# Layer 0 of a hybrid decoder step: decode states, cache rows and decode queries put between the units of the latent prompt attention

## The chip, the cores and the metric

The kernel runs on one core of a Trainium2 chip. The metric is device time in microseconds (us) of one launch. The kernel before was timed three times: 3633.6 us in the median, 3632.26 to 3640.36.

A core has four compute engines, each with its own list of instructions that it works off in order: TensorE (PE: matmuls and transposes, results in PSUM), VectorE (DVE), ScalarE (ACT) and GpSimd (POOL, here mostly a queue for indirect DMAs). SyncE (SP) issues the other DMAs. Engines wait for each other by semaphores. PSUM has eight banks of 128 x 512 float32, here `ps[:, 0]` to `ps[:, 7]`.

## The reference

One inference step of a two-layer trunk over a prompt of 1024 tokens and 8 decode tokens (one for each of 8 running sequences). The change lies in layer 0, which runs latent attention (MLA, 8 heads) beside gated linear attention (GLA, 4 heads), for the prompt and for the decode tokens:

```
q_pe  = rope(q[..., 64:], pos)
q_lat = einsum('bqhc', q[..., :64], w_uk)            # queries into the latent space
c_kv  = rms_norm(kv_a[..., :256]); k_pe = rope(kv_a[..., 256:])
rows  = concat([c_kv, k_pe])                         # cache rows, an output (prompt and decode)
keys  = rows                     (prompt)   or  concat([cache[page_table], rows])   (decode)
mla   = softmax(scale * (q_lat . c_kv + q_pe . k_pe), causal) . c_kv . w_uv
o, s_fin = gla_chunked(gq, gk, gv, log_a, s0)        # s = exp(last) * s + k^T v;  s_fin is an output
o     = rms_norm(o, g_norm) * silu(g_r)
out   = concat([mla, o]) @ w_out
```

For a decode token GLA is one step: the state read from memory is scaled by the decay, the outer product of key and value is added (`s_fin`), and the output is the query times the new state.

## The kernel before, in words

All data live in one SBUF array (`arena`). `NT` = 8 is the number of 128-token tiles, `NH` = 8 the heads of MLA, `DEC` = 8 the decode tokens, `SEQ` = 1024, `T` = 1032. Instructions are written in program order, engine by engine; there is no scheduler. `link` makes an engine wait for its own last result; `enter(e, k)` makes it wait until every engine has reached phase k, and `leave` counts the phase up: an engine barrier.

Layer 0 runs, after the input projection, in these parts:

- `pe_gla` and its partners: 16 steps of the GLA recurrence over the prompt, with the projections of the MLA queries between them (`QH`). After each chunk `gnorm(n)` normalises its output: ScalarE squares, TensorE sums over partitions in bank 7 (line 1051), ScalarE takes Ln and Exp, each of which loads its own function table (lines 1062 and 1064), and VectorE multiplies (1069, 1073).
- Then, one after the other: the decode keys (two transposes, 1154; VectorE spreads them by token, 1185), `gnorm(7)`, 4 value units (`pe_mla_values`, 1280: a tile of 128 tokens times `w_uv`, into banks 6 and 7, copied by VectorE at 1287), the decode states (16 matmuls, 1167, over banks 1 to 4, each followed by two VectorE operations, 1195), 4 more value units, the decode outputs (32 matmuls of one column, 1177), the cache rows (9 tiles, three transposes each, 1220 and 1221, copied at 1241 and sent out by SP), the decode queries (24 matmuls, 1225), the transposed new row (1230), and `gnorm(8)` for the decode tokens.
- Phase 8, a barrier of all engines, then `pe_mla`, `act_mla`, `dve_mla`: the prompt attention. POOL passes the same barrier and issues the first two page gathers of the decode attention behind it.
- Phase 9, the decode attention over the paged cache (`pages`).

The attention works through `MU`, 64 units (head, query tile), in the order 0, 7, 1, 6, 2, 5, 3, 4 of the query tiles, so small and large units take turns. Unit u with query tile i has i + 1 key tiles. Its steps are: `scores(u)` (TensorE, banks 0 and 1 or 2 and 3, line 1311), `mask(u)` (VectorE adds the causal mask and takes the maximum, 1404, 1407), the exponential (ScalarE, 1375), `turn(u)` (TensorE transposes the weights into banks 4 and 5, 1323), `finish(u)` (VectorE copies them into the single buffer `PT`, 1421), `values(u)` (TensorE, bank 6 or 7, 1335) and the output (ScalarE, 1371). TensorE issues, for each u, `scores(u + 1)`, `turn(u)`, `values(u - 1)`. Keys of a head (`keys(h)`, four matmuls of 128x512, 1296, copied at 1394) use banks 4 and 5 too. The names `turn(1)`, `scores(0)` and so on below mean these steps with their unit number, over all heads: u = 8 is the first unit of the second head.

SP issues in layer 0, in this order: GLA's prompt states, the decode states, the eight prompt row tiles, the decode row, and then (after the scores of the decode attention) the input again and the weights of the next projection.

## Time and profile before

| | us |
|---|---|
| median of three timed runs | 3633.6 |
| the profiled execution, its own time | 3640.52 |
| its span in the trace | 3638.7 |
| TensorE matmul busy | 3399.5 (93%) |
| VectorE busy | 1668.2 (46%) |
| ScalarE busy | 630.5 (17%) |
| mean granted TensorE clock | 0.968 |

The profile is one execution. Times within it count from the start of the span. PE is TensorE's matmuls, PEld its weight loads, which overlap them. A float32 matmul leaves two records in the trace, so counts of records are twice the counts of instructions. Clock is what the throttle granted to TensorE as a share of 2.4 GHz. In a timeline row the first number is the start, the second how long the group lasted; `[1.13 <-ACT ...]` is the idle time of that engine before it, and what ended it.

### The profile page before, as it was taken

Reading aid. Unit: us, or ns where it says so; the run is one execution under the profiler, and the core shown is the slowest. Engines: PE = TensorE matmul, PEld = TensorE weight load, DVE = VectorE, ACT = ScalarE, POOL = GpSimd, SP = SyncE. Lnnn points to the kernel's source line nnn. Section 1 sums busy time; section 2 is a strip of 40 time slices with the busy share of each in tenths; the row PEclk is TensorE's granted clock in tenths of the full one; section 3 lists DMA queues with packets and bytes.
Section 4 is the critical chain, followed back from the end, with each engine's and each line's share of the span. In section 5 each row is a group of like instructions: output and inputs, shape, how many; then the busy total and the mean of one; then the engine's idle time right before and its main releaser. Section 6 shows DMA issues by size and latency. Waiting matters only on the chain. (4 is left out here: it accounts for less than half of the span.)

```text
span 3638.7 us, 45085 instructions
## 1 busy us (share of the span) xinstructions
PE 3399.5 (93%) x18216; PEld 2510.8 (69%) x18216; DVE 1668.2 (46%) x3894; ACT 630.5 (17%) x1628; POOL 95.0 (3%) x138
## 2 busy tenths in 40 slices
PE   9999888766889999999999999999987999999997
PEld 5675565654557777776777767767764777777676
DVE  0216455688254333357760212122456433335777
ACT  1214223233130000000030111111223000000002
POOL 0000000011000000000000000000220000000000
PEclk9999799899899999999999999999988999999998
DMA  3120100298321111111221111122210111011122
GB/s 134 35 58 1 46 33 1 108 351 325 128 82 47 46 37 43 46 61 64 78 87 46 60 56 55 56 73 69 79 67 23 47 46 46 35 46 61 64 89 100
DMA packets 63531, 266.58 MB, mean 73 GB/s; under 512 B 6288, under 2 KB 24728, under 8 KB 52352
## 3 DMA queue, kind: packets, MB, share of 16 engines
q1 hardware_dynamic: 55072, 176.94, 14.0%
q0 software_dynamic: 8288, 87.30, 6.4%
q8 instruction: 114, 1.87, 0.2%
q14 instruction: 57, 0.47, 0.0%
HBM read 246.29 MB, written 17.93 MB: 73 GB/s over the span
## 5 line engine op out<-in xcount | busy, mean ns | idle before, releaser
L512 PE MATMUL ps<-arena 128*128 128x344 f32 (+1 forms) x4928 | 1083.1, 383 | 22.4 <-ACT arena L560 12.0
L512 PEld LDWEIGHTS ps<-arena 128*128 128x128 f32 x4928 | 833.6, 192 | 272.6 <-issue 26.0
L766 PE MATMUL ps<-arena 128*128 128x344 f32 (+1 forms) x2464 | 539.8, 382 | 1.5 <-DVE arena L685 1.5
L766 PEld LDWEIGHTS ps<-arena 128*128 128x128 f32 x2464 | 415.3, 191 | 126.7 <-DVE arena L685 3.4
L1945 PE MATMUL ps<-arena 128*128 128x344 f32 x1152 | 354.3, 465 | 15.6 <-ACT arena L352 5.7
L1945 PEld LDWEIGHTS ps<-arena 128*128 128x128 f32 x1152 | 221.3, 195 | 134.7 <-issue 26.3
L216 PE MATMUL ps<-arena 128*128 128x344 f32 x672 | 198.5, 459 | 8.9 <-DMA arena<-in_w_a 8.9
L1956 PE MATMUL ps<-arena 128*128 128x256 f32 (+1 forms) x864 | 206.4, 396 | 0.0
L1956 PEld LDWEIGHTS ps<-arena 128*128 128x128 f32 (+1 forms) x864 | 178.9, 264 | 23.5 <-issue 6.2
L562 ACT ACTIVATE arena<-arena 128x688 f32<-128x688 f32 (+1 forms) x88 | 55.7, 633 | 756.5 <-DVE arena L624 756.5
L216 PEld LDWEIGHTS ps<-arena 128*128 128x128 f32 x672 | 129.8, 194 | 76.8 <-DMA arena<-in_w_a 8.9
L1656 DVE STREAM_TRANSPOSE arena<-arena 128x1152 f32<-128x1152 f32 x128 | 167.6, 1352 | 21.9 <-DMA arena<-in_cache,arena 21.9
L1530 PE MATMUL ps<-arena 128*32 128x128 f32 x2304 | 77.2, 293 | 56.1 <-DVE arena L1656 56.1
L2094 ACT ACTIVATE arena<-arena 128x128 f32<-128x128 f32 (+1 forms) x192 | 84.0, 438 | 244.6 <-DVE arena L2137 244.6
L2132 DVE CUSTOM_DVE_ANT_0 arena<-ps,arena 128x128 f32<-128x128 f32 (+1 forms) x192 | 56.1, 348 | 136.0 <-PE ps L2052 89.3
L374 PE MATMUL ps<-arena 128*128 128x344 f32 x384 | 115.0, 462 | 0.8 <-DVEq L155 0.8
L1530 PEld LDWEIGHTS ps<-arena 128*32 128x32 f32 x2304 | 67.5, 119 | 64.5 <-DVE arena L1656 63.7
L2000 DVE COPY arena<-ps 128x344 f32<-128x344 f32 x36 | 18.5, 516 | 194.1 <-PE ps L1945 194.1
L374 PEld LDWEIGHTS ps<-arena 128*128 128x128 f32 x384 | 74.6, 195 | 40.0 <-issue 2.4
L598 DVE TENSOR_TENSOR arena<-arena 128x512 f32<-128x512 f32 x44 | 30.4, 692 | 151.9 <-DMA arena<-in_w_fi 151.9
L621 DVE TENSOR_TENSOR arena<-arena,ps 128x344 f32<-128x344 f32 (+1 forms) x88 | 37.2, 423 | 109.0 <-PE ps L512 109.0
L624 DVE TENSOR_TENSOR arena<-arena,ps 128x344 f32<-128x344 f32 (+1 forms) x88 | 37.2, 423 | 108.9 <-PE ps L512 108.9
(322 smaller groups left out, 3662.0 us busy)
## 6 DMA issues: line engine op xcount, KB each, us to landing
arena<-in_w_fi SPq DMA_DIRECT2D x44, 1024.0 KB, 4.8
arena<-in_w_fo SPq DMA_DIRECT2D x16, 1536.0 KB, 6.4
arena<-in_w_fo SPq DMA_DIRECT2D x16, 1280.0 KB, 5.7
arena<-in_w_out_a SPq DMA_DIRECT2D x24, 512.0 KB, 3.5
arena<-in_w_qk SPq DMA_DIRECT2D x24, 512.0 KB, 3.6
arena<-in_c SPq DMA_DIRECT2D x6, 2048.0 KB, 12.3
arena<-in_x SPq DMA_DIRECT2D x6, 1376.0 KB, 10.3
arena<-in_w_a SPq DMA_DIRECT2D x14, 512.0 KB, 3.5
```

The source lines that it names most:

```text
L216: mm = pe.matmul(ps[:, 3 * u + c, 0:C], w[:, k, :], X[:, k, chunk(c)], start=(k == 0), stop=(k == KD - 1))
L374: mm = pe.matmul(ps[:, 3 * u + s // 2 % 3, 0:C], w[:, k, :], rhs(k)[:, chunk(c)], start=(k == 0), stop=(k == kt - 1))
L512: mm = pe.matmul(ps[:, BANK[p], 0:HALF[s]], prod[j][p][0], prod[j][p][1], start=(j == 0), stop=(j == 3))
L562: act.activation(GATE[:, 0:2 * HALF[s]], GATE[:, 0:2 * HALF[s]], ACT.Silu).then_inc(st_g, 1)
L621: dve.tensor_tensor(v, u, bank["p7"], ALU.add).then_inc(st_e, 1)
L766: mm = pe.matmul(ps[:, BANK[p], 0:HALF[s]], prod[p][0], prod[p][1], start=(j == 0), stop=(j == NKP - 1))
L1530: mm = pe.matmul(ps[32 * j:32 * j + 32, n % 2, 0:P], QBD[n // NG % 2][:, cb, :], KVT[(4 * n + j) % 8][:, :, cb * 32:cb * 32 + 32], start=( ...
L1656: dve.transpose(KVT[(4 * n + q) % 8], KV[n % 4][:, 4 * q:4 * q + 4, :]).then_inc(kt_done, 1)
L1945: mm = pe.matmul(ps[:, b, 0:C], w[:, k, :], X[:, k, chunk(c)], start=(k == 0), stop=(k == KD - 1))
L1956: mm = pe.matmul(ps[0:P if tt < NT else DEC, b, 0:256], X[:, k, block_slice(g, tt)], w[:, k, :], start=(k == 0), stop=(k == KD - 1))
L2094: act.activation(DS[n % 2][:, j, 0:nk], DS[n % 2][:, j, 0:nk], ACT.Exp, bias=DMX[:, n % 2, j:j + 1], scale=DIL_SCALE, accum_out=s[:, 260 + ...
L2132: dve.tensor_tensor_reduce(DS[n % 2][:, j, 0:nk], ps[:, j % 2, off:off + nk], BIAS[i % 2][:, j, 2 * P - nk:2 * P], 1.0, NEG, ALU.add, ALU. ...
```

## The change

The barrier in front of phase 8 is gone: after GLA TensorE goes straight on with `keys(0)`. All steps on decode states, cache rows and decode queries move out of the stretch in front of the attention and become fills inside it. `FILL` lists them: `("keys", 0)`, 8 times `state`, 2 times `out`, `norm`, 9 times `row`, `query` and `new`, 23 entries. Entry k stands at unit u = 2k + 2, behind `values(u - 1)` on TensorE and behind `finish(u)` on VectorE; ScalarE's part of the norm stands behind the exponential of the odd unit after it.

So that the attention keeps banks 0 to 6, all fills share bank 7, and `values(u)` has bank 6 alone, so it waits for the output of u - 1 (before: of u - 2). A state step handles one token: two matmuls into bank 7, four VectorE operations. The decode outputs are two steps of 16 matmuls. The decode queries of GLA are copied to a small place (`GQD`) first, since the attention's output `O` goes over them; the key buffers `KH` and the row buffers `KVROW` have new places. The value units (6, then 2) and `gnorm(7)` stand in front of scores(0), between keys(0) and keys(1). The page gathers wait for nine output transfers (GLA's prompt states, decode states, and the decode row) in place of the barrier and eight.

```diff
         def pe_gla_decode_keys(pe):
-            pe.wait_ge(g_atc, NGLU)
+            pe.wait_ge(gn_r, NT)
+            pe.wait_ge(v_cp, NT)
             for pr in range(2):
-                mm = pe.transpose(ps[0:DEC, 0, pr * P:pr * P + P], gk[:, pr, SEQ:T], ident[:, :])
+                mm = pe.transpose(ps[0:DEC, 7, pr * P:pr * P + P], gk[:, pr, SEQ:T], ident[:, :])
...
+        def pe_gla_decode_state(pe, b):
+            pe.wait_ge(gs_km, b + 1)
+            if b:
+                pe.wait_ge(gs_stc, 2 * b)
+            for pr in range(2):
+                pe.matmul(ps[:, 7, 2 * pr * P:2 * pr * P + 2 * P], KM[0:DEC, b, pr * P:pr * P + P],
+                          GV[0:DEC, NT, 2 * pr * P:2 * pr * P + 2 * P], start=True, stop=True).then_inc(gs_st, 1)
+        def pe_gla_decode_out(pe, hh):
+            pe.wait_ge(gs_stc, 2 * DEC)
+            if hh:
+                pe.wait_ge(gs_o, 2)
+            r = slice(64 * hh, 64 * hh + 64)
+            for pr in range(2):
+                for b in range(DEC):
+                    mm = pe.matmul(ps[:, 7, pr * DEC + b:pr * DEC + b + 1], SG[r, b, pr, :], GQD[r, pr, b:b + 1],
+                                   start=True, stop=True)
+            mm.then_inc(gs_o, 1)
...
+        FILL = [("keys", 0)] + [("state", b) for b in range(DEC)] + [("out", 0), ("out", 1), ("norm", 0)]
+        FILL += [("row", tt) for tt in range(NT + 1)] + [("query", 0), ("new", 0)]
+        def fill_at(u):
+            return FILL[u // 2 - 1] if u % 2 == 0 and 0 < u // 2 <= len(FILL) else ("", 0)
...
             def values(u):
-                if u >= 2:
-                    pe.wait_ge(m_oc, u - 1)
+                if u:
+                    pe.wait_ge(m_oc, u)
...
             keys(0)
+            pe.wait_ge(gn_r, NT - 1)
+            pe_mla_values(pe, range(6))
+            pe.wait_ge(v_cp, 6)
+            pe_gnorm(pe, NT - 1)
+            pe.wait_ge(kh_cp, 1)
+            keys(1)
+            pe.wait_ge(gn_r, NT)
+            pe_mla_values(pe, range(6, NT))
+            scores(0)
             for u, (h, i) in enumerate(MU):
...
                 if u:
                     values(u - 1)
+                fill(*fill_at(u))
...
+                if u and fill_at(u - 1) == ("out", 1):
+                    act.wait_ge(gs_o, 4)
+                    act_gnorm_squares(act, NT)
+                if u and fill_at(u - 1) == ("norm", 0):
+                    act_gnorm(act, NT)
...
             for u, (h, i) in enumerate(MU):
                 if u + 1 < len(MU):
                     mask(u + 1)
                 finish(u)
+                fill(*fill_at(u))
+                if u and fill_at(u - 1) == ("norm", 0):
+                    link("dve", dve, dve_gnorm(dve, NT))
...
             pool.wait_ge(pidx_ok, NG)
-            enter(pool, 8)
-            pool.wait_ge(out_done, 16 * 8)
+            pool.wait_ge(out_done, 16 * 9)
             gather(0)
```

Where the instructions stand. TensorE before, from the end of GLA to the first row tiles (1154 decode keys, 1051 norm, 1280 values, 1167 states, 1177 outputs, 1220 and 1221 rows):

```order
152 L1041 MATMUL ps<-arena 128x256
153 L1154 MATMUL ps<-arena 8x128 x2
154 L1051 MATMUL ps<-arena 128x512
155 L1280 MATMUL ps<-arena 128x512 x8
156 L1167 MATMUL ps<-arena 128x256 x16
157 L1280 MATMUL ps<-arena 128x512 x8
158 L1177 MATMUL ps<-arena 128x1 x32
159 L1220 MATMUL ps<-arena 128x128 x2
160 L1221 MATMUL ps<-arena 128x32
161 L1220 MATMUL ps<-arena 128x128 x2
162 L1221 MATMUL ps<-arena 128x32
```

and, further on in the same list, from the last row to the first turn (1225 queries, 1230 new row, 1296 keys, 1311 scores, 1323 turn):

```order
175 L1220 MATMUL ps<-arena 8x128 x2
176 L1221 MATMUL ps<-arena 8x32
177 L1225 MATMUL ps<-arena 96x8 x16
178 L1225 MATMUL ps<-arena 64x8 x8
179 L1230 MATMUL ps<-arena 96x8 x3
180 L1051 MATMUL ps<-arena 128x32
181 L1296 MATMUL ps<-arena 64x512 x4
182 L1311 MATMUL ps<-arena 128x128
183 L1296 MATMUL ps<-arena 64x512 x4
184 L1311 MATMUL ps<-arena 128x512 x2
185 L1323 MATMUL ps<-arena 128x128
```

TensorE after, the whole way from the end of GLA to the first turns (1309 is keys, 1293 values, 1324 scores, 1336 turn, 1348 values(u)):

```order
152 L1041 MATMUL ps<-arena 128x256
153 L1309 MATMUL ps<-arena 64x512 x4
154 L1293 MATMUL ps<-arena 128x512 x12
155 L1051 MATMUL ps<-arena 128x512
156 L1309 MATMUL ps<-arena 64x512 x4
157 L1293 MATMUL ps<-arena 128x512 x4
158 L1324 MATMUL ps<-arena 128x128
159 L1324 MATMUL ps<-arena 128x512 x2
160 L1336 MATMUL ps<-arena 128x128
161 L1324 MATMUL ps<-arena 128x256
162 L1336 MATMUL ps<-arena 128x128 x8
163 L1348 MATMUL ps<-arena 128x64
```

Everything between the last GLA matmul (1041) and keys(0) has left; the values and the norm come behind keys(0), and 25 matmuls stand between GLA and scores(0).

TensorE after, around the first state steps (1157 decode keys, 1165 a state step, units u = 2 to 4):

```order
166 L1336 MATMUL ps<-arena 128x128 x2
167 L1348 MATMUL ps<-arena 128x64 x8
168 L1157 MATMUL ps<-arena 8x128 x2
169 L1324 MATMUL ps<-arena 128x384
170 L1336 MATMUL ps<-arena 128x128 x7
171 L1348 MATMUL ps<-arena 128x64 x2
172 L1324 MATMUL ps<-arena 128x512
173 L1324 MATMUL ps<-arena 128x256
174 L1336 MATMUL ps<-arena 128x128 x3
175 L1348 MATMUL ps<-arena 128x64 x7
176 L1165 MATMUL ps<-arena 128x256 x2
```

Each fill stands between the values of the odd unit before it and the scores of the next but one.

VectorE before, from the last GLA norm but one to the second block of values (1069 and 1073 norm, 1183 and 1185 decode keys, 1287 value copies, 1195 states):

```order
148 L1069 SCALAR_TENSOR_TENSOR arena<-arena 128x512
149 L1073 TENSOR_TENSOR arena<-arena 128x4x128
150 L1183 COPY arena<-ps 8x256
151 L1185 TENSOR_SCALAR arena<-arena 8x256 x8
152 L1069 SCALAR_TENSOR_TENSOR arena<-arena 128x512
153 L1073 TENSOR_TENSOR arena<-arena 128x4x128
154 L1287 COPY arena<-ps 128x512 x4
155 L1195 SCALAR_TENSOR_TENSOR arena<-arena,ps 64x128 x32
156 L1287 COPY arena<-ps 128x512 x4
```

VectorE after, around the decode keys (1480 the copy of the turned weights, 1181 and 1183 the decode keys, 1191 a state step, 1463 and 1466 the mask, 1475 the reciprocal):

```order
175 L1480 COPY arena<-ps 128x256
176 L1181 COPY arena<-ps 8x256
177 L1183 TENSOR_SCALAR arena<-arena 8x256 x8
178 L1463 ISA arena<-ps,arena 128x384
179 L1463 ISA arena 128x1
180 L1466 TENSOR_SCALAR arena<-arena 128x1
181 L1475 RECIPROCAL arena<-arena 128x1
182 L1480 COPY arena<-ps 128x896
183 L1463 ISA arena<-ps,arena 128x768
184 L1463 ISA arena 128x1
185 L1466 TENSOR_SCALAR arena<-arena 128x1
186 L1475 RECIPROCAL arena<-arena 128x1
```

The nine operations of the decode keys now stand in front of mask(4); before they stood in front of `gnorm(7)` and all value copies.

## Rows read from the trace of the kernel before

**Rows 1.** Windows by stage: length, busy time (instructions) per engine, clock, DMA, GB/s

```profile
385.00:447.00 62.00, 54.27 (x214) 33.78 (x211) 28.35 (x73) 8.19 (x11) 0.00 (x0) 0.67 0.14 39
447.00:489.00 42.00, 36.72 (x141) 22.78 (x142) 18.07 (x47) 9.29 (x25) 2.54 (x2) 0.77 0.28 113
489.00:517.00 28.00, 24.78 (x141) 16.69 (x140) 15.09 (x41) 8.77 (x24) 0.00 (x0) 1.00 0.00 1
517.00:685.00 168.00, 151.19 (x856) 104.70 (x855) 91.53 (x245) 52.43 (x143) 0.00 (x0) 0.97 0.00 1
```

**Rows 2.** Timeline, GLA's end: start, us, engine, line, op, idle before

```profile
384.21 0.83 PE L1041 MATMUL ps<-arena 128*128 128x256 f32 x2 [1.55 <-ACT arena L1087]
...
386.21 2.08 PE L1051 MATMUL ps<-arena 128*128 128x512 f32 x2 [0.75 <-ACT arena L1056]
...
391.01 9.04 PE L1280 MATMUL ps<-arena 128*128 128x512 f32 x16 [2.72 <-ACT arena L1064]
...
394.83 0.69 DVE L1287 COPY arena<-ps 128x512 f32<-128x512 f32 x1 [2.36 <-PE ps L1280]
```

**Rows 3.** Timeline, decode and cache steps up to the attention

```profile
387.82 2.18 DVE L1185 TENSOR_SCALAR arena<-arena 8x256 f32<-8x256 f32 x8
...
399.98 11.60 PE L1167 MATMUL ps<-arena 8*128 8x256 f32 x32
...
400.78 11.79 DVE L1195 SCALAR_TENSOR_TENSOR arena<-arena,ps 64x128 f32<-64x128 f32 x32
...
420.47 6.75 PE L1177 MATMUL ps<-arena 64*128 64x1 f32 x64
...
428.01 0.69 PE L1220 MATMUL ps<-arena 128*128 128x128 f32 x2
...
428.88 0.69 PE L1220 MATMUL ps<-arena 128*128 128x128 f32 x2
...
436.35 7.08 PE L1225 MATMUL ps<-arena 64*96 64x8 f32 x48
...
444.68 1.28 ACT L1064 ACT_TABLE_LOAD   x1
445.97 0.23 ACT L1064 ACTIVATE arena<-arena 128x32 f32<-128x32 f32 x1
...
446.99 6.56 PE L1296 MATMUL ps<-arena 128*64 128x512 f32 x8 [2.65 <-DVEq L2756]
```

**Rows 4.** Timeline, scores(1) and turn(1) of the first head

```profile
458.85 1.99 PE L1311 MATMUL ps<-arena 96*128 96x512 f32 x4
...
463.62 1.97 PE L1323 MATMUL ps<-arena 128*128 128x128 f32 x8 [2.25 <-ACT arena L1375]
```

**Rows 5.** Windows, turn(1) to the next keys, first and second head

```profile
463.62:488.73 25.11, 23.38 (x115) 18.55 (x115) 11.74 (x32) 7.50 (x21) 0.00 (x0) 0.74 0.00 1
497.08:516.63 19.55, 17.46 (x115) 13.44 (x115) 11.66 (x32) 7.47 (x22) 0.00 (x0) 1.00 0.01 1
```

**Rows 6.** Timeline, TensorE's waits in the second head

```profile
497.08 1.09 PE L1323 MATMUL ps<-arena 128*128 128x128 f32 x8 [1.13 <-ACT arena L1375]
...
514.07 0.74 PE L1323 MATMUL ps<-arena 128*128 128x128 f32 x5 [0.67 <-DVE arena L1421]
...
516.63 3.65 PE L1296 MATMUL ps<-arena 128*64 128x512 f32 x8 [0.98 <-DVE arena L1421]
```

**Rows 7.** Windows of 2 us around changes of the granted clock

```profile
384.00:386.00 2.00, 1.26 (x4) 0.52 (x4) 0.81 (x3) 0.99 (x4) 0.00 (x0) 0.66 0.00 0
394.00:396.00 2.00, 2.00 (x4) 0.79 (x4) 0.69 (x1) 0.00 (x0) 0.00 (x0) 0.78 0.00 0
422.00:424.00 2.00, 2.00 (x27) 2.00 (x27) 0.00 (x0) 0.00 (x0) 0.00 (x0) 1.00 0.00 0
424.00:426.00 2.00, 2.00 (x22) 2.00 (x22) 0.00 (x0) 0.00 (x0) 0.00 (x0) 0.90 0.00 0
440.00:442.00 2.00, 2.00 (x15) 1.98 (x15) 0.00 (x0) 0.00 (x0) 0.00 (x0) 0.50 0.00 0
```

More of the change, by code:

```diff
@@ L1331, in values, with fill @@
                     pe.wait_ge(v_cp, NT)
-                if u >= 2:
-                    pe.wait_ge(m_oc, u - 1)
+                if u:
+                    pe.wait_ge(m_oc, u)
                 for j in range(i + 1):
-                    mm = pe.matmul(ps[:, 6 + u % 2, 0:64], PT[:, j * P:(j + 1) * P], V[:, j, h * 64:h * 64 + 64],
+                    mm = pe.matmul(ps[:, 6, 0:64], PT[:, j * P:(j + 1) * P], V[:, j, h * 64:h * 64 + 64],
                                    start=(j == 0), stop=(j == i))
                 mm.then_inc(m_o, 1)
-            keys(0)
+            def fill(what, x):
+                if what == "keys":
+                    pe_gla_decode_keys(pe)
+                if what == "state":
+                    pe_gla_decode_state(pe, x)
+                if what == "out":
+                    pe_gla_decode_out(pe, x)
+                if what == "norm":
+                    pe_gnorm(pe, NT)
+                if what == "row":
+                    pe_cache_row(pe, x)
+                if what == "query":
+                    pe_decode_query(pe)
+                if what == "new":
+                    pe_decode_row(pe)
+            pe.wait_ge(q_act, 3 * NH)
+            pe.wait_ge(q_dve, 3 * NH)
+            keys(0)
+            pe.wait_ge(gn_r, NT - 1)
[6 more added lines that the diff above has]
+            pe_mla_values(pe, range(6, NT))
+            pe.wait_ge(g_atc, NGLU)
+            pe.wait_ge(g_oc, NGLU)
+            pe.wait_ge(g_stc, NGLU)
+            scores(0)
             for u, (h, i) in enumerate(MU):
-                if u == 0:
-                    scores(0)
-                    pe.wait_ge(kh_cp, 1)
-                    keys(1)
                 if u + 1 < len(MU):
@@ L1388, in dve_mla, with fill @@
             for q in range(2):
-                dve.wait_ge(row_out[q], 16 * (NT // 2))
-            for q in range(2):
                 dve.tensor_copy(KH[q][64:96, :], PB[64:96, T_MISC, 0:SEQ]).then_inc(kh_pe, 1)
+            dve.tensor_copy(GQD, gq[:, :, SEQ:T])
+            def fill(what, x):
+                if what == "keys":
+                    dve_gla_decode_keys(dve)
+                if what == "state":
+                    dve_gla_decode_state(dve, x)
+                if what == "out":
+                    dve_gla_decode_out(dve, x)
+                if what == "row":
+                    dve_cache_row(dve, x)
+                if what == "query":
+                    dve_decode_query(dve)
+                if what == "new":
+                    dve_decode_row(dve)
             def keys(h):
@@ L2643, in _ @@
             pe_gla(pe)
[L2644 to L2654 removed]
             pe.sem_inc(phase["pe"], 8)
[L2656 to L2658 removed]
+            pe_mla(pe)
+            enter(pe, 9)
+            pe_pages(pe)
             enter(pe, 10)
```

171 lines of the change are left out of this document (68 added, 103 removed).

## The prediction

> **What bounds the kernel now.** I read the windows by stage first, then the timeline of layer 0 from the end of the gated linear attention (GLA) into the latent prompt attention, then the granted clock around it. The change touches the stretch from 385 to 685 us only, and there TensorE sets the pace in all of it: it is busy 54.3 of 62 us between the GLA and the attention, and 151 of 168 us in the attention [rows 1]. But the first stretch is busy at a mean clock of 0.67 and the rest at 0.97 to 1.00 [rows 1]. As the clock has two levels (1.0 is 2.4 GHz, 0.5 is 1.2 GHz), 0.67 means that about 41 of the 62 us ran at half speed. So the stretch holds three kinds of time: work that the attention needs first (16 value matmuls), decode and cache work that nothing in the prompt attention reads, and idle time at hand-overs.
>
> GLA's last matmul ends at 385.04 [rows 2]; turn(1), the first transposes of a large unit, starts at 463.62 [rows 4]. I use turn(1) as the mark, since from it on both kernels run the same loop.
>
> **The prologue: what goes.** Between the marks lie 78.6 us. They hold the norm's matmul at 386.21 and the idle stretch to 391.01 [rows 2]; decode states 11.6 us; decode outputs 6.75 us; nine cache rows at 0.86 us each (the distance of two) at half clock; decode queries 7.1 us; then a tail without dense work, from 443.4 to 446.95, in which ScalarE loads a table and all engines meet [rows 3]; and keys(0) at half clock, 6.56 us instead of 3.65 [rows 3, 6].
>
> **The prologue after.** TensorE's list is keys(0), six value units, the norm's matmul, keys(1), two value units, scores(0), scores(1). At full clock keys take 3.65 us, in 8 records (two for each 128x512 float32 matmul), so 0.43 us a record when they follow each other [rows 6]; a value unit is two matmuls, 4 records, 1.71 us. Nothing holds keys(0) back: its queries are done in GLA. Sum: keys 2 x 3.43 = 6.9; values 8 x 1.71 = 13.7; norm 0.9. One wait is exposed: the norm's matmul writes bank 7, so it waits for the copy of value 5, about 0.9 us (the copy is 0.69 us [rows 2], the rest is the hand-over). The next wait, ScalarE's Ln and Exp on that norm, was 2.7 us of TensorE idle at 391.01 [rows 2]; now keys(1), 3.4 us, lies under it. The clock fell at the end of GLA (0.66 in 384 to 386) and rose 3.9 us after dense matmuls began at 391.01 [rows 2, 7]. I assume the same: 3.9 us at half from 385, which costs 2.0. So scores(0) start at 385.1 + 6.9 + 13.7 + 0.9 + 0.9 + 2.0 = 409.5, and scores(1) at 409.9. Before, scores(1) started at 458.85 and turn(1) 4.77 us later [rows 4]; that piece (mask, exp, then the idle 2.25 us) does not change. turn(1): about 414.6. **Gain of the prologue: 49 us.** Bounds: clock full at once, 51; clock half through all of it, 23 us of work twice as long, 49 - 21 = 28. I take the row's 3.9 us, as the list is dense 128-row work like that at 391.
>
> **The loop: what comes.** A fill stands behind values(u-1) at each even u. Its work on TensorE is paid in full unless TensorE waited next. In a head at full clock (19.55 us from turn(1) to the next keys [rows 5]) the waits are 1.13 us in front of the turn of the second unit, 0.67 in front of the last unit's, and 0.98 in front of keys [rows 6]; a fill at u%8=0 lies under the first, one at u%8=6 under the second. Fills at 2 and 4 lie under nothing. Terms:
> - 8 state steps at u = 4 to 18: two matmuls of 256 columns, each half of a keys matmul, 0.91 us per step. Gross 7.3. Hidden: twice 0.67 and twice 0.91, 3.2. VectorE's four operations (0.37 each, 11.79/32 [rows 3]) come in front of the next mask and PT copy; laid into a head they push the copy by 0.2 to 0.4 us, 8 x 0.25 = 2.0. The first steps run at half clock, +0.9. Net 7.0.
> - keys step, u = 2: two transposes 0.6 us; VectorE's 2.2 us [rows 3] fall where TensorE is slow. 0.6.
> - two output steps: 64 records, 27 in 2 us at full clock [rows 7], 4.7 us; 0.67 hidden. 4.1.
> - norm step: ScalarE loads two tables, 1.28 us each [rows 3], with two short operations 3.1 us, in front of the exp of u = 26 and of VectorE's norm, which stands before mask(27). Between 0 (the exp of u = 26 is small and early) and 3.1 (all of it late) I take 1.3, as a small unit's exp is wanted only after a large unit's turn and values.
> - 9 row steps at u = 26 to 42: 0.43 us (half of 0.86), 3.9; four lie under waits. 2.2.
> - query step, u = 44: 48 records at 27 in 2 us, 3.6, nothing hides it. (At half clock it took 7.1 [rows 3].) The last step, 0.2, is hidden.
> Sum 18.8 us. The single output bank adds a wait of values(u) for output(u-1), but ScalarE does that output right after exp(u+1), and turn(u+1), at least 0.3 us, stands between. I cost it at 0; if it came out it would be 0.3 us in 64 units, 19.
>
> The ACT_TABLE_LOAD is also where a page speaks against the change: "ScalarE: Activation LUTs" of the Trainium skill, section on what the load costs, puts 1.38 us of drain behind each, 2.66 in all. The row shows the next ACTIVATE 0.01 us after the load ends (444.68 + 1.28, 445.97 [rows 3]). By the page the norm step would cost 2.8 us more; I follow the row.
>
> **The clock in the loop.** The decode outputs started at full clock and it fell 5 us into them (0.90 in 424 to 426), and it stayed at 0.50 while they, the rows and the queries kept TensorE busy 2.00 of 2.00 us [rows 7]. So small matmuls (few rows or columns) don't hold the clock, busy or not. An output step is 2.4 us and the query step 3.6, shorter than those 5, with attention between. One half-clock spell is priced by the first head: 25.11 us at a mean clock of 0.74 against 19.55 at 1.00, thus 5.6 us for 13 us at half, 0.43 us per us [rows 5]. That spell began in the idle of turn(1), and I leave it in both kernels. I add one spell of 9 us for the outputs or the query, 4 us. "TensorE: Matmul & The Clock Gate" in the Trainium skill (What's actually happening) says that busyness releases the throttle. By that alone I would add nothing; the row at 440 to 442, busy and at half, disagrees.
>
> **DMA and POOL.** The first two page gathers wait now for nine output transfers, the last of which (the new cache row) goes out at u = 42 of 64. Some 22 units at 3.5 us, 77 us, remain before the pages stage. The gathers are the DMA of 447 to 489, 0.28 of 42 us, 12 us [rows 1]. Hidden, cost 0. SP has in front of the pages stage only output transfers, so its later queue is not late.
>
> **Sum.** 49 - 18.8 - 4 = 26, with a unit of doubt in each step; I take 27, as the fill at u%8=6 also shortens the idle that ends heads, before two of which the clock fell (0.97 in 517 to 685 [rows 1]). The profiled execution took 3640.5 us (span 3638.7 and 1.8 around it), so 3613.5 by its own measure. It is 6.9 us above the median of the timed runs, 3633.6, which gives **3607 us** for the median.
>
> **Rivals.**
> 1. *The clock doesn't hold (ends slower).* Fills of 8-row and 1-column matmuls keep TensorE at half in the 46 units that have them. For it: the fall at 425 and the half clock at 440 [rows 7]. Against it: dense scores between, and keys each head. Each us at half costs 0.43, so the 30 us left after the fills are gone at 70 us of added half clock. In the limit, 5.75 heads of 28 us stretched by 1/(1 - 0.43), +120 us less the first 5.6: about 3715. A part of it (20 to 60 us at half) gives 3612 to 3629.
> 2. *VectorE becomes the bound.* It is busy 15 of 28 us in a head [rows 1]; a head with four state steps needs 21. If all its added work came on the path (32 x 0.37, 2.2 + 0.4, 9 x 0.46 and 1 us, 19.5 us) beside TensorE's, 3607 + 17 = 3624. Against it: after each even unit it has a short copy and then waits for TensorE.
> 3. *More is won.* TensorE's fills end the idle on which the clock fell at turn(1) and at the ends of heads, and there is no added spell: 27 + 5.6 + 4 = 37, 3597.
> 4. *It doesn't do what it says*: the gathers or one semaphore of the last steps come late and the pages stage waits for them, up to 12 us: 3619.
>
> **Chances.** Forecast (3600 to 3615) 0.63; rival 1 in part 0.12, in full with more than 70 us 0.04; rival 2, 0.08; rival 3, 0.10; rival 4, 0.03. Two medians here can be told apart from about 0.2%, 7 us. Slower than 3641: 0.04. Within 7 us: the far part of rivals 1 and 2, 0.05. Faster: 0.91. The range 3596 to 3622 leaves out the far part of rivals 1 and 2 and beyond 3.
>
> **What would show it.** scores(0) near 410 and turn(1) near 415; a head with state steps 2 to 4 us longer than 28; TensorE waiting for VectorE's state operations nowhere; the granted clock at 1.00 from about 389 to 412; gathers near 590 us and no wait for them behind 660; the pages stage as long as before. A prologue that ends past 425, or heads over 33 us, makes the forecast wrong.

## The result and the profile after

The changed kernel takes 3619.35 us in the median of 11 runs (3611.86 to 3630.63), against 3632.62 us of the kernel before in 11 runs (3627.24 to 3641.59) on the same chips. The ratio is 0.9966, 95% interval 0.9957 to 0.9976: 13 us faster (by the interval 9 to 16). Forecast were 27 us, and a range of 3596 to 3622. The direction and the mechanism held, and the gain was half of the forecast.

The profiled execution took 3621.58 us with a span of 3619.8, so it is near its median, while that of before was 8 us above its own. The traces differ by 18.9 us: 13.9 of it is there when the attention ends (the first output transposes start at 667.72 instead of 681.59), and 5 us come later, in stages that the change doesn't touch. The medians show 13.3, so I count with the 13.9.

**The prologue.** Timeline of the changed kernel on TensorE, from the end of GLA to turn(1) (1309 is keys, 1051 the norm, 1324 scores, 1336 turn; six value units stand between the first two rows); it answers to [rows 2, 4]:

```profile
385.08 4.93 PE L1309 MATMUL ps<-arena 128*64 128x512 f32 x8
...
401.29 0.30 PEld L1051 LDWEIGHTS ps<-arena 128*128 128x128 f32 x2 [1.61 <-DVE arena L1300]
401.29 1.12 PE L1051 MATMUL ps<-arena 128*128 128x512 f32 x2 [0.79 <-DVE arena L1300]
...
409.46 2.10 PE L1324 MATMUL ps<-arena 96*128 96x128 f32 x6
...
414.35 1.39 PE L1336 MATMUL ps<-arena 128*128 128x128 f32 x8 [2.24 <-ACT arena L1415]
```

keys(0) follow GLA without a gap, the only waits are 0.79 us for value 5's copy and the 2.24 us in front of turn(1), and turn(1) starts at 414.35 instead of 463.62: 49.3 us gained, 49 forecast.

**The loop.** Windows of the changed kernel: the prologue, the first head from turn(1) to the next keys, and the third, fourth and sixth from keys to keys (columns as in [rows 1]; the clock is the third number from the end). They answer to [rows 1, 5]:

```profile
385.00:414.35 29.35, 26.33 (x60) 9.89 (x59) 15.52 (x31) 6.67 (x11) 0.00 (x0) 0.95 0.02 5
...
414.35:445.36 31.01, 28.40 (x126) 21.74 (x126) 16.86 (x49) 7.50 (x21) 0.00 (x0) 0.68 0.01 1
...
478.05:518.98 40.93, 39.34 (x213) 30.15 (x213) 18.11 (x51) 9.30 (x25) 0.00 (x0) 0.86 0.12 27
518.98:551.16 32.18, 29.08 (x152) 18.72 (x152) 16.80 (x46) 11.74 (x28) 0.00 (x0) 0.92 0.04 15
...
579.52:612.93 33.41, 31.46 (x197) 22.85 (x198) 16.84 (x48) 8.95 (x24) 2.13 (x2) 0.95 0.37 147
```

From turn(1) to the end of the last unit the loop lasts 253.4 us instead of 218.0. So 35.4 of the 49.3 us are paid back in it, 22.8 were forecast (18.8 for the fills, 4 for one clock spell). By heads, with half-clock time as 2 x (1 - clock) x length:

| head | before, us | after, us | added | half clock before | after |
|---|---|---|---|---|---|
| 1 (from turn(1)) | 25.11 | 31.01 | 5.9 | 13.1 | 19.8 |
| 2 | 27.90 | 32.69 | 4.8 | 0 | 3.9 |
| 3 | 27.53 | 40.93 | 13.4 | 0 | 11.5 |
| 4 | 27.54 | 32.18 | 4.6 | 0 | 5.1 |
| 5 | 27.54 | 28.36 | 0.8 | 0 | 0 |
| 6 | 27.57 | 33.41 | 5.8 | 0 | 3.3 |
| 7, 8 | 54.78 | 54.79 | 0 | 6.6 | 6.6 |

The half-clock time grows by 30.5 us. At 0.43 us each (the price from [rows 5]) that is 13 us, where one spell of 9 us was forecast. 10.6 of the 30.5 lie in heads 1 and 2, in front of the first output step, and 19.9 in heads 3, 4 and 6, which hold the output and query steps or stand right behind them. The largest single loss is the third head, with the two output steps. Timeline of the changed kernel there (1175 is an output step, 1309 the next keys):

```profile
498.26 5.13 PE L1175 MATMUL ps<-arena 64*128 64x1 f32 x32
...
510.64 3.96 PE L1175 MATMUL ps<-arena 64*128 64x1 f32 x32
...
518.98 6.24 PE L1309 MATMUL ps<-arena 128*64 128x512 f32 x8 [0.98 <-DVE arena L1480]
```

and windows of 1 us in the same place:

```profile
499.00:500.00 1.00, 1.00 (x11) 1.00 (x10) 0.00 (x0) 0.00 (x0) 0.00 (x0) 1.00 0.92 220
...
501.00:502.00 1.00, 1.00 (x7) 1.00 (x6) 0.00 (x0) 0.00 (x0) 0.00 (x0) 0.50 0.03 10
...
514.00:515.00 1.00, 1.00 (x6) 0.98 (x6) 0.17 (x1) 0.15 (x1) 0.00 (x0) 0.50 0.09 16
```

The first step begins at full clock, which falls in the middle of it (0.67 in 500 to 501) and is back in 507 to 508; the second loses it at 514, near its end, and the keys behind it, 6.24 us instead of 3.65, are still at half for the most part. The clock is at half from 602.6 to 606 too, right behind the query step (3.91 us, 598.40). In the first head it falls at about 428, in the first state step and 2 us behind the wait in front of turn(3), and stays at half for 20 us.

Other lines of the changed kernel on which steps of the forecast rested: turn(3) behind the decode keys step, a table load of the norm and the turn behind it, the first page gather and the query step (1336 turn, 1062 the norm on ScalarE, 1222 the query):

```profile
425.80 0.52 PE L1336 MATMUL ps<-arena 128*128 128x128 f32 x3 [1.62 <-DVE arena L1480]
...
530.08 1.28 ACT L1062 ACT_TABLE_LOAD   x1
...
533.75 0.44 PE L1336 MATMUL ps<-arena 128*128 128x128 f32 x2 [1.01 <-ACT arena L1415]
...
595.91 1.16 POOL L1566 DMA_INDIRECT arena<-in_cache,arena  x1 [595.46 <-DMA out_mla_s<-arena]
...
598.40 3.91 PE L1222 MATMUL ps<-arena 64*96 64x8 f32 x48
```

TensorE waits 1.62 us for the copy that stands behind VectorE's nine decode-key operations. The tables cost 1.28 us each, and the turn behind them waits 1.01 us. The gathers go out at 596 and are long over when the pages stage starts at 674.6.

### The profile page after: what moved, and what is told of

Its sections match the earlier page's. It is cut to its first block and busy times, and to the rows that moved or that the text cites. A ratio compares the mean times of both kernels' runs of the same rounds, so it can differ in the third digit from the quotient of the medians.

```text
span 3619.8 us, 45102 instructions
## 1 busy us (share of the span) xinstructions
PE 3392.2 (94%) x18216; PEld 2503.9 (69%) x18216; DVE 1667.2 (46%) x3895; ACT 631.0 (17%) x1628; POOL 94.4 (3%) x138
## 5 line engine op out<-in xcount | busy, mean ns | idle before, releaser
L512 PE MATMUL ps<-arena 128*128 128x344 f32 (+1 forms) x4928 | 1082.7, 383 | 22.4 <-ACT arena L560 12.0
L766 PEld LDWEIGHTS ps<-arena 128*128 128x128 f32 x2464 | 414.6, 190 | 127.6 <-DVE arena L685 3.4
L2023 PEld LDWEIGHTS ps<-arena 128*128 128x128 f32 (+1 forms) x864 | 178.7, 263 | 23.7 <-issue 6.2
## 6 DMA issues: line engine op xcount, KB each, us to landing
arena<-in_x SPq DMA_DIRECT2D x6, 1376.0 KB, 10.2
```

What stands on the lines that cost most here:

```text
L512: mm = pe.matmul(ps[:, BANK[p], 0:HALF[s]], prod[j][p][0], prod[j][p][1], start=(j == 0), stop=(j == 3))
L766: mm = pe.matmul(ps[:, BANK[p], 0:HALF[s]], prod[p][0], prod[p][1], start=(j == 0), stop=(j == NKP - 1))
L2023: mm = pe.matmul(ps[0:P if tt < NT else DEC, b, 0:256], X[:, k, block_slice(g, tt)], w[:, k, :], start=(k == 0), stop=(k == KD - 1))
```

## The experiments

The theory after the result: **runs of matmuls that use little of the array (one column, eight columns) make the granted clock fall, and the dense work behind them pays.** Its rivals: the fills' own work or VectorE's part was priced too low; the fills stand at the wrong units; the delay itself shifts the loop against whatever lowers the clock. Times are medians; each ratio is against runs of the kernel before in the same job, whose medians were 3633.72, 3633.56 and 3636.88 us in the three jobs. Half-clock totals are for the loop of one profiled execution (before 19.7, changed kernel 50.2). Such a total belongs to that execution, which can lie 5 us and more off the median of its kernel: e1_thin, e2_slots and e10_wide_slots were profiled in the fastest of their executions, e6_dense in the slowest.

### e1_thin: output and query steps cut down

```diff
-                for b in range(DEC):
+                for b in range(1):
                     mm = pe.matmul(ps[:, 7, pr * DEC + b:pr * DEC + b + 1], SG[r, b, pr, :], GQD[r, pr, b:b + 1],
...
-                for h in range(NH):
+                for h in range(1):
                     mm = pe.matmul(ps[0:m, 7, (ct * NH + h) * DEC:(ct * NH + h + 1) * DEC], w_ukT[0:64, h, ct * 96:ct * 96 + m],
```

This kernel leaves out the outputs of seven of the eight tokens and the queries of seven of the eight heads.

> The changed kernel with the two decode output steps cut to one of eight columns per head pair and the decode query step to one of eight heads; all steps, copies and waits stay (decode outputs and queries are not computed in full). In the changed kernel these steps took 5.13 + 3.96 + 3.91 us. Theory 1 (clock): these runs of small matmuls also make the granted clock fall, at 500.7, 514 and about 610 us, and what follows runs at half. Then the kernel gains the steps' own 12 us and some 5 us of spells: 3602, and the third head (478 to 519 us) drops from 40.9 to about 29 us. Theory 2 (work only): the clock falls anyway, on the free-running idle at head ends: gain 9 us (the steps at full clock), 3610, and the half-clock time in the loop stays at about 55 us.

Measured: 3600.98 us, ratio 0.9908 (0.9895 to 0.9920), so 33 us under before and 18 under the changed kernel, where the work-only theory expected 9. The work cut is about 9.5 us at full clock (two output steps from 3.73 us, see e2_slots, to 0.60; the query step from 3.91 to 0.71), so some 9 us are clock. Windows of its heads 1 to 3:

```profile
414.54:440.61 26.07, 24.45 (x125) 18.85 (x125) 16.76 (x49) 7.39 (x21) 0.00 (x0) 0.80 0.01 2
440.61:471.43 30.82, 29.04 (x156) 19.79 (x157) 20.45 (x57) 8.79 (x24) 0.00 (x0) 1.00 0.00 1
471.43:501.19 29.76, 28.18 (x156) 19.52 (x156) 17.93 (x51) 9.19 (x25) 0.00 (x0) 1.00 0.16 36
```

Only the first head has half-clock time, 10.4 us; all heads behind it run at 1.00. The output and the query steps are gone, and with them the spells of heads 3, 4 and 6. The DMA is not what made them: it is as busy here in heads 3 and 6 (0.16 and 0.39 of the time; 0.12 and 0.37 in the changed kernel). Two limits. This execution (3594.41 us) was the fastest of its five, 6.6 us under their median; at 0.43 that is an estimate of 15 us more at half clock in the typical one. And the eight state steps (8 rows, 256 columns) and nine row steps, which are all still there, do no harm in this execution, but spells of 3 to 10 us begin in or right behind a state step in others: e11_late, e8_spread and e6_dense have them in heads without any output or query step. This run also measures the fills at full clock: head 2 has four state steps and is 2.9 us longer than before (forecast 3.05), head 4 has the norm and three rows, 2.0 longer (1.3 + 0.9 forecast).

### e6_dense: the same time on TensorE, but dense

In e1_thin, in front of each of the three cut steps, four matmuls whose result is not used:

```diff
+            for _ in range(4):
+                pe.matmul(ps[:, 7, :], ident[:, :], PB[:, T_CKV, 0:512], start=True, stop=True)
```

> e1_thin (output and query steps cut to a few matmuls) with four 128x512 matmuls on 128 rows put in front of each of the three cut steps, 3.4 us each, so TensorE is held as long as by the full steps, but with dense work. Theory 1 (small matmuls drop the clock, time held does not): 10 us longer than e1_thin, 3611, and no half-clock time behind the three steps (total in the loop as in e1_thin, about 10 us, all in the first head). Theory 2 (any delay of 3 to 5 us shifts the loop against whatever drops the clock): spells of 3 to 7 us behind the steps as in the changed kernel, 3616 or more.

Measured: 3611.26 us, ratio 0.9934 (0.9918 to 0.9950), 10 us over e1_thin as theory 1 has it, and 8 us under the changed kernel (the intervals of the two ratios don't overlap), though its three steps hold TensorE about 1 us longer than the full ones do at full clock (2 x 3.73 + 3.91). The first of the three steps (1174 the dense matmuls, 1177 what is left of the outputs), and the windows of heads 3 and 6:

```profile
499.18 3.65 PE L1174 MATMUL ps<-arena 128*128 128x512 f32 x8
502.76 0.60 PE L1177 MATMUL ps<-arena 64*128 64x1 f32 x4
```

```profile
479.07:515.63 36.56, 34.97 (x172) 22.20 (x173) 18.12 (x51) 9.19 (x25) 0.00 (x0) 1.00 0.13 29
...
573.57:605.61 32.04, 30.10 (x163) 19.73 (x163) 16.85 (x48) 8.84 (x24) 2.13 (x2) 1.00 0.38 153
```

TensorE is held 4.2 us there and the clock stays at 1.00 through both heads. The delay is not what lowers it: the shape of the work in the delay counts. The total half-clock time is 33.9 us and not 10, from 27 us in heads 1 and 2, where this kernel is identical to e1_thin, and 6.6 at the end. So that part of the expectation was wrong: spells there come and go between executions of the same instructions. The lengths check the price: this loop is 21.0 us longer than e1_thin's (246.2 and 225.2); 3 x 3.6 us of dense work and 23.5 us of half clock at 0.43 give 20.9. The two traces lie on opposite sides of their medians, though (this one, 3616.14 us, is the slowest of four), which is why they differ by twice the 10 us of the medians.

### e7_dve: VectorE's state operations cut to 4 columns

```diff
-   out=SG[r, b, pr, :], in0=SG[r, b, pr, :], ..., in1=ps[r, 7, (2 * pr + hh) * P:(2 * pr + hh + 1) * P]
+   out=SG[r, b, pr, 0:4], in0=SG[r, b, pr, 0:4], ..., in1=ps[r, 7, (2 * pr + hh) * P:(2 * pr + hh) * P + 4]
```

Of each decode state only 4 of the 128 columns are updated here.

> The changed kernel with VectorE's 32 state operations cut from 128 columns to 4 (the decode states are computed only there). If VectorE's work in front of masks and copies costs as forecast, 2 us come back: 3617. Rival: VectorE is a main part of the missing gain (each operation's 0.35 us on the path in half the steps, 6 us or more): 3613 or less. Neither expects the half-clock time behind the outputs and queries to change.

Measured: 3622.23 us, ratio 0.9969 (0.9957 to 0.9981), the same as the changed kernel. Window of head 2:

```profile
445.22:476.86 31.64, 30.58 (x156) 20.14 (x156) 18.76 (x57) 8.65 (x24) 0.00 (x0) 0.95 0.00 1
```

Head 2, with its four state steps and 3.2 us at half, is 31.6 us against 32.7: VectorE's operations cost at most 1 us per head with four of them, near the forecast and no part of the miss. The third head drew 22.5 us of half clock in this execution instead of 11.5, which hides what the four state steps there save.

### e2_slots: the fills behind the units that TensorE waits after

```diff
-            return FILL[u // 2 - 1] if u % 2 == 0 and 0 < u // 2 <= len(FILL) else ("", 0)
+            return FILL[AT.index(u)] if u in AT else ("", 0)
+        AT = [2, 6, 7, 8, 14, 15, 16, 22, 23, 24, 30, 31, 32, 37, 38, 39, 40, 45, 46, 47, 48, 55, 56]
```

> The same 23 fills, at other units: u = 2, then behind the units that TensorE waits after (u mod 8 = 6, 7, 0 for the state and output steps, 5, 6, 7, 0 for the rows). Theory 1 (clock falls on small matmuls): total work is the same, waits of 0.4 to 1.1 us are filled, some 8 us are hidden, but half-clock spells stay as long: 3611. Theory 2 (the fills at units 2 and 4 cost in full and the idle at head ends sets the clock): filled idle also removes falls, the loop loses 13 us or more: 3605 or less. Rival: VectorE at consecutive units is late with masks and copies: no gain, 3619 or slower, with TensorE waiting for VectorE's copy of the turned weights over 10 us more than before.

Measured: 3615.28 us, ratio 0.9944 (0.9932 to 0.9956). Windows of head 2 and of the stretch with the outputs:

```profile
436.93:465.29 28.36, 27.95 (x153) 18.79 (x153) 19.27 (x54) 8.68 (x24) 0.00 (x0) 1.00 0.00 1
...
493.90:537.03 43.13, 42.44 (x208) 31.34 (x207) 17.09 (x47) 9.97 (x26) 0.00 (x0) 0.74 0.11 25
```

TensorE's waits by what ended them, from 415 to 640 us (total, times, longest), of this kernel (1337 turn, 1310 keys):

```profile
PE ps L1337 <- DVE arena L1481: 2.7, 4, 1.6
PE ps L1337 <- ACT arena L1416: 1.8, 3, 0.6
PE ps L1310 <- DVE arena L1481: 1.8, 3, 0.6
```

and of the changed kernel, from 415 to 668 us (1309 keys, 1336 turn):

```profile
PE ps L1309 <- DVE arena L1480: 6.1, 6, 1.2
PE ps L1336 <- ACT arena L1415: 5.3, 6, 1.1
PE ps L1336 <- DVE arena L1480: 4.5, 8, 1.6
```

The waits shrink from 15.9 to 6.3 us (7.3 when counted to the end of the loop at 657), and head 2 is 28.4 us, 4.3 less; it holds three state steps instead of four, and no half-clock time instead of 3.9 us. But the head with the outputs now holds 22.4 us at half and the last two, with the query, 17.5, 48 us in all, as many as in the changed kernel. (6 of the 22.4 belong to a spell that began at 492.5, in the state step in front.) The first theory had forecast that the spells stay, and 3611. The medians show 4 us of its 8, the ratios against before 8.

The second output step runs at full clock to its end here, which gives its price:

```profile
529.55 3.73 PE L1175 MATMUL ps<-arena 64*128 64x1 f32 x32
```

### e3_split: outputs in four pieces, queries in three

```diff
-        def pe_gla_decode_out(pe, hh):
+        def pe_gla_decode_out(pe, q):
...
+            hh, pr = divmod(q, 2)
             r = slice(64 * hh, 64 * hh + 64)
-            for pr in range(2):
-                for b in range(DEC):
+            for b in range(DEC):
...
-        def pe_decode_query(pe):
+        def pe_decode_query(pe, x):
...
-            for ct in range(3):
+            for ct in (x,):
...
+        FILL = [("keys", 0)] + [("state", b) for b in range(DEC)] + [("out", q) for q in range(4)] + [("norm", 0)]
+        FILL += [("row", tt) for tt in range(NT + 1)] + [("query", ct) for ct in range(3)] + [("new", 0)]
```

> The changed kernel with the two output steps as four of eight matmuls and the query step as three of eight, so 27 steps at even units up to 54. No run of small matmuls is longer than about 1.5 us. If the length of the run is what drops the clock, the spells behind the outputs and the query go: third head shorter, 3612. If not (the share of small matmuls over a longer time counts, or the clock falls on idle), the time stays within 3 us of 3619.

Measured: 3612.27 us, ratio 0.9944 (0.9931 to 0.9957), 7 us under the changed kernel by the medians; by the intervals of the ratios, they only touch. Windows of heads 3 and 4 (outputs) and the last two (queries):

```profile
473.02:506.58 33.56, 32.22 (x180) 23.56 (x181) 18.23 (x51) 8.96 (x24) 0.00 (x0) 0.93 0.14 32
506.58:541.82 35.24, 33.35 (x177) 23.04 (x177) 16.32 (x46) 12.09 (x29) 0.00 (x0) 0.87 0.02 5
...
600.21:654.99 54.78, 50.87 (x331) 37.86 (x331) 29.82 (x83) 17.38 (x47) 2.03 (x2) 1.00 0.22 87
```

The query pieces keep full clock (1.00 in the last two heads). The two heads with the output pieces hold 14 us at half, against 17 in the changed kernel; 3.4 of them begin at 488, behind a state step and before the first piece (494.45), the rest behind pieces. So the length of one run is not all of it.

### e5_slots_split and e8_spread: both moves together

e3_split with e5's list (below); e8_spread has the same pieces at AT = 2, 6, 7, 8, 14, 15, 16, 22, 23, 24, 30, 32, 38, 39, 40, 45, 46, 47, 48, 50 to 54, 56, 58, 60:

```diff
-            return FILL[u // 2 - 1] if u % 2 == 0 and 0 < u // 2 <= len(FILL) else ("", 0)
+            return FILL[AT.index(u)] if u in AT else ("", 0)
+        AT = [2, 6, 7, 8, 14, 15, 16, 22, 23, 24, 30, 31, 32, 37, 38, 39, 40, 45, 46, 47, 48, 49, 50, 53, 54, 55, 56]
```

> Both moves together: the fills behind the units that TensorE waits after (e2_slots) and the outputs and queries in pieces of eight matmuls (e3_split), the three queries at units 53, 54, 55 and the outputs at 24, 30, 31, 32. If the two gains add (waits filled: loop 7 us shorter than the change at full clock; shorter runs: 16 us less at half clock, 7 us), about 3605 against 3612 to 3615 for each alone. If small matmuls close together act like one long run, the clock falls behind units 30 to 32 and 53 to 55 and the time is that of e2_slots, 3615.

> As e5_slots_split, but the pieces lie apart: outputs at units 24, 30, 32, 38, queries at 54, 56, 58. If closeness is what drops the clock, this one keeps it where e5 loses it: 3602 and under 15 us at half clock in the loop. If only the single run's length counts, it equals e5 within 3 us.

Measured: 3612.65 us, ratio 0.9943 (0.9931 to 0.9956), and 3609.58 us, 0.9931 (0.9918 to 0.9944). The gains don't add. Windows of e8, heads 4 and 5:

```profile
502.43:534.12 31.69, 30.63 (x172) 22.77 (x172) 17.06 (x47) 8.88 (x24) 0.00 (x0) 0.90 0.15 35
534.12:567.46 33.34, 32.65 (x175) 23.21 (x175) 15.62 (x43) 9.74 (x26) 0.00 (x0) 0.86 0.00 0
```

Their loops hold 57 and 54 us at half clock, more than the changed kernel's. In e8, 10 of them begin at 466, right behind a state step, before any output piece. e8 lies 3 us below e5, within what can't be told apart, and far from the 15 us at half that it was to show. Neither the length nor the distance of the runs cures it; filling TensorE's waits with the same pieces saves the waits, and there was no less half clock with it.

### e4_serial: no barrier, no fills

The prologue of the changed kernel, with the decode, cache and query steps in one piece in the form and the banks of the kernel before:

```diff
             keys(1)
+            pe_gla_decode_keys(pe)
             pe.wait_ge(gn_r, NT)
             pe_mla_values(pe, range(6, NT))
...
+            pe_gla_decode_states(pe)
+            pe_gla_decode_out(pe)
+            pe_cache_rows(pe)
...
             scores(0)
...
-                fill(*fill_at(u))
```

> Only the first half of the change: no barrier, keys(0), six value units, the norm, keys(1) and two value units first, but then all decode states, outputs, rows and queries in one piece in front of scores(0), over several banks as in the kernel before; no fills in the loop. Work of 35 us at mostly half clock behind 410 us: scores(0) at about 445 instead of 454.85, loop as before, gain 9 us: 3624. So interleaving alone would be worth 4 us of the measured 13. Rival: the serial piece runs at full clock and takes under 28 us, then it is as good as the change (3619 or less).

Measured: 3628.27 us (12 runs), ratio 0.9983 (0.9974 to 0.9992): 5 to 6 us gained, not 9. Its timeline on TensorE (1170 states, 1180 outputs, 1327 turn) and the window of the serial piece:

```profile
412.78 11.96 PE L1170 MATMUL ps<-arena 8*128 8x256 f32 x32 [0.70 <-DVE arena L1188]
425.67 11.33 PE L1180 MATMUL ps<-arena 64*128 64x1 f32 x64 [0.93 <-DVE arena L1198]
...
461.57 1.97 PE L1327 MATMUL ps<-arena 128*128 128x128 f32 x8 [1.72 <-ACT arena L1396]
```

```profile
409.00:457.00 48.00, 44.37 (x189) 32.96 (x188) 21.56 (x63) 3.31 (x5) 2.13 (x2) 0.59 0.30 95
```

turn(1) starts at 461.6, 2 us earlier than before. The piece runs at a mean clock of 0.59: the outputs, at full clock for most of their 6.75 us before [rows 3, 7], take 11.33 us here. Putting the value units first took away the dense work in the middle of the decode steps, in which the clock had come back before (at about 415, in the second block of value units). So without interleaving the change is worth 5 to 6 us, and the fills as they are bring 6 to 9 more (6 by the ratios, 9 by the medians).

### e9_wide: the outputs with the states streaming

The 16 queries of a head pair (two heads, eight tokens) stand as columns of a 128x128 tile `QM`, zero where a query doesn't belong to the half of the rows. For each token its 16 columns are the weights, and the 128-row state streams through, summed in PSUM. The second step turns the 16x128 results.

```diff
             for pr in range(2):
-                for b in range(DEC):
-                    mm = pe.matmul(ps[:, 7, pr * DEC + b:pr * DEC + b + 1], SG[r, b, pr, :], GQD[r, pr, b:b + 1],
-                                   start=True, stop=True)
+                if hh:
+                    mm = pe.transpose(ps[:, 7, 16 * pr:16 * pr + 16], OT[0:16, pr, :], ident[0:16, 0:16])
+                else:
+                    for b in range(DEC):
+                        mm = pe.matmul(ps[0:16, 7, pr * P:pr * P + P], QM[:, pr, 16 * b:16 * b + 16], SG[:, b, pr, :],
+                                       start=(b == 0), stop=(b == DEC - 1))
```

> The changed kernel, its decode outputs computed another way: the 16 queries of a head pair stand as 16 columns (zero where they don't belong), the states stream through as 128 columns on 128 rows, summed over the tokens; 16 matmuls in the first step, two 16-row transposes in the second, in place of 32 matmuls of one column. If the one-column matmuls drop the clock (and cost 9.1 us), the two spells behind units 20 and 22 go: third head from 40.9 to about 32 us, median 3610. If any matmul that uses the array little drops it, only work is saved: 3614.

Measured: 3609.37 us, ratio 0.9930 (0.9917 to 0.9944). Both steps (1177, 1174), and the windows of heads 3 and 6:

```profile
492.81 3.67 PE L1177 MATMUL ps<-arena 128*16 128x128 f32 x32
...
501.87 0.29 PE L1174 MATMUL ps<-arena 16*128 16x16 f32 x2
```

```profile
472.66:505.44 32.78, 30.94 (x182) 21.68 (x182) 18.30 (x51) 9.14 (x25) 0.00 (x0) 1.00 0.14 33
...
564.91:602.96 38.05, 36.47 (x198) 27.12 (x198) 16.84 (x48) 8.96 (x24) 2.13 (x2) 0.79 0.33 129
```

The third head has no half-clock time and is 32.8 us instead of 40.9. The steps themselves took 3.96 us instead of 9.09; against the 7.46 that two of them take at full clock (2 x 3.73), 3.5 us are work and the rest is clock. By the medians the gain over the changed kernel is 10 us, so some 6 of them are clock. Head 6, with the unchanged query step, drew 16 us at half in this execution (3.3 in the changed kernel's).

### e10_wide_slots: e9_wide with e2_slots' list AT

```diff
-            return FILL[u // 2 - 1] if u % 2 == 0 and 0 < u // 2 <= len(FILL) else ("", 0)
+            return FILL[AT.index(u)] if u in AT else ("", 0)
```

> e9_wide with the fills at the units of e2_slots (behind u mod 8 = 6, 7, 0, rows also 5), the query at unit 55. Waits filled (7 to 9 us in e2_slots at full clock) and the outputs' spells gone add: 3603. If the fills close together drop the clock by themselves, it stays at 3610.

Measured: **3596.79 us, ratio 0.9897 (0.9882 to 0.9912)**, 37 us under before by the ratio and the fastest version of the study. Windows from turn(1): head 1, heads 2 and 3, the last two:

```profile
412.85:434.55 21.70, 19.63 (x126) 14.95 (x126) 15.35 (x46) 7.38 (x21) 0.00 (x0) 1.00 0.01 2
434.55:491.45 56.90, 56.19 (x304) 37.62 (x305) 38.55 (x106) 17.35 (x48) 0.00 (x0) 0.99 0.00 1
...
579.99:640.12 60.13, 55.98 (x335) 41.10 (x335) 30.33 (x85) 17.61 (x47) 2.13 (x2) 0.91 0.21 82
```

The first head never falls (21.7 us against 31.0), the heads with states hold 0.99, and the whole loop has 18 us at half, less than before the change. The profiled execution (3587.78 us) was the fastest of its four, 9 us below their median, so the typical loop has more half clock than 18 us. The expectation was 3603.

### e11_late: the first head without fills

```diff
+            return FILL[AT.index(u)] if u in AT else ("", 0)
+        AT = [8, 10, 12, 14, 16, 18, 20, 22, 24, 26, 28, 30, 32, 34, 36, 38, 40, 42, 44, 46, 48, 50, 52]
```

This one reads the decode keys after the attention's output has gone over them, so its decode states are those of other numbers; the work is the same.

> The changed kernel with every fill 6 units later (u = 8 to 52), so the first head, in which the clock falls in every trace, has none. If fills in that head prolong its half-clock time (19.8 us against 13.1 before), it goes back to about 13 us and 25 us in length, and the kernel gains up to 4 us: 3615. If the length of that spell varies by itself, the time is 3619 within 2 us.

Measured: 3616.43 us, ratio 0.9951 (0.9937 to 0.9965). The first head:

```profile
413.37:433.99 20.62, 18.89 (x116) 14.78 (x116) 11.74 (x32) 7.28 (x21) 0.00 (x0) 0.91 0.01 2
```

The first head is 20.6 us with 3.7 us at half, better than the 25.1 before, but the fills it doesn't have cost in later heads. The medians differ by 3 us, less than can be told apart. Heads 2 and 3 of this kernel hold the keys step, seven state steps and nothing else, and still have 6.8 and 6.7 us at half; head 2:

```profile
433.99:468.05 34.06, 31.16 (x155) 20.86 (x155) 21.57 (x62) 8.84 (x24) 0.00 (x0) 0.90 0.00 0
```

The half-clock time of the first head varies by itself: e1_thin and e6_dense, identical up to there, have 10.4 and 20.6 us. But the fills are not cleared of a part in it. The six traces with fills at units 2, 4 and 6 have 10.2, 10.4, 13.5, 19.8, 20.6 and 20.6 us; the other seven (no fill in this head, or the keys step at 2 and states at 6 and 7) have 0, 3.2, 3.7, 3.7, 10.4, 12.9 and 13.1. That speaks for a part of the fills and doesn't show it.

## Why the prediction was off

- **Prologue: right.** Forecast scores(0) at 409.5 and turn(1) at 414.6, seen 409.46 and 414.35; the clock rose sooner than 3.9 us (keys(0) took 4.93 us, 1.3 over full speed, 2.0 forecast).
- **State, row and norm steps: right.** Four state steps 2.9 us (3.05 forecast), four rows 0.8 us in head 5 (0.86), the norm about 1.2 (1.3). VectorE is not the bound (e7_dve). The rival of the late gathers did not come.
- **The output steps: mis-sized work.** 64 records were priced at 27 in 2 us [rows 7], 4.7 us. A window counts a record that crosses its edge in both neighbours, so 27 was too many: the group began at 420.47 and some 58 of its 64 records had begun when the clock fell 5 us later, 0.09 us each, 5.6 for all. As a fill the same work is slower still, 3.73 us for each step at full clock (e2_slots), 7.5 for both. So the term is 2.8 us short; why the steps are slower in the loop is open. The query step is 0.3 short (3.91 us at full clock, 3.6 forecast).
- **The decode keys step:** forecast 0.6 us, as the first head was thought to be at half. It was at full clock there, and TensorE waited 1.62 us for VectorE; in e11_late, which has no keys step there, it doesn't wait. About 1 us.
- **The step that failed is the clock in the loop.** The forecast saw that small matmuls don't hold the clock, noted that it fell 5 us into the outputs, and concluded that steps of 2.4 and 3.6 us, being shorter, would be mostly safe: one spell of 9 us, 4 us of time. In the trace both output steps and the query step lose it, before they end or right behind, and what follows (turns, values, the next keys) pays: 19.9 us at half in heads 3, 4 and 6, 8.6 us of time instead of 4. Three runs bear it out in the medians: e1_thin takes the steps out, e6_dense puts equal time of dense work in their place, e9_wide does the output sum with wider matmuls, and each gains some 9, 9 and 6 us beyond the work that it changes.
- **The first two heads.** The forecast left their half-clock time as it was. It rose from 13.1 to 23.7 us, 4.6 us of time. This is not the output or query steps, which come later; part of it is the draw of one execution (e6_dense against e1_thin), part may be the fills there (e11_late).
- **The account of the loop.** It cost 12.6 us more than forecast. 4.6 are the spells of outputs and query, 4.6 those of the first two heads, 4.1 the three sizes above. That is 0.7 us too much; the price of 0.43 is rough.
- In chances, rival 1 "in part" (20 to 60 us at half, 3612 to 3629) is what happened. It had 0.12. The row that spoke for it, busy 2.00 of 2.00 us at 0.50 [rows 7], was read rightly and then given too small a place. "TensorE: Matmul & The Clock Gate" in the Trainium skill (What's actually happening) says that activity releases the throttle. By that alone the spells in the output and query steps should not be there. The trace disagrees: TensorE was busy 1.00 of 1.00 us at 0.50 in 501 to 502, and the dense steps of e6_dense, as long, kept 1.00. It is not busyness alone.

What stays open: why the same instructions at the start of the attention get 10 to 21 us at half clock in different executions, what part the state steps have in the spells that begin in or behind them, and 5 us that the two profiled executions differ by behind the attention. It was also not tried to compute the query step in a wider form.

## What to carry to other kernels

Small matmuls moved into a dense TensorE loop cost their own time and, if they use few columns, the clock of the dense work behind them. Price them by the granted clock of a stretch that holds them, and check whether the same sum can be written with the large operand streaming. Then put fills behind the units that the engine waits after: here that gave 4 us by the medians with the small matmuls (e2_slots) and 13 us on top of e9_wide without the one-column ones (e10_wide_slots). By the ratios it is 8 and 12, with intervals that overlap, so that the two moves help each other is not shown.

## What the runs showed of the hardware

- 32 one-column matmuls (64 weight loads of 64x128): in one group before, 58 records begun in 5 us at full clock; as two fills 3.73 us each at full clock (e2_slots, 529.55). The first fill began at 498.26 at full clock, and from 501 on it ran at 0.50. The same products as 16 matmuls of 128 columns and 16 weights took 3.67 us, with 1.00 throughout.
- Eight-row matmuls with 256 columns left the clock at 1.00 over heads 2 and 3 in one execution (e1_thin); with seven such steps and the decode keys step there it was 0.90 in both heads in another (e11_late). In one unbroken run of 11.6 us before, it had fallen (0.78 in the 2 us from 404).
- An activation table load costs 1.28 us with the next operation 0.01 us behind it (before, 444.68 and 445.97), and 0.02 us in the loop (530.08 and 531.38).
